# Hybrid pool / SGU / cross-attention layer on 8 cores: a new order of first loads and statistics, and four tiles of x transposed by DMA

## Chip, cores and metric

The kernel runs on the 8 cores of one Trainium2 chip. Each core computes one half (2048 rows) of one of the four sequences and no core waits for another. The metric is the device time in microseconds of the slowest core. All figures of the profile are of core 4, the slowest in the profiled execution.

## What is computed

```python
h    = rmsnorm(x, norm_pre)                       # (B, S, 2048)
proj = h @ w_in                                   # columns: xa | ga | u | v | gb | q | gc, 1024 each
ya = pool_mixer(xa) * silu(ga)
yb = u * (tril(W_s) @ layernorm(v) + b_s) * silu(gb)      # in chunks of 128 positions, 8 heads
yc = softmax(q k^T / 16) v_mem * silu(gc)                 # 4 heads, 256 memory tokens
y  = concat(rmsnorm(ya), rmsnorm(yb), rmsnorm(yc))
out = x + rmsnorm(y @ w_out, norm_post)
```

The change touches the first stage only: h, its transpose hT (kept on chip for all later projections), v = h @ w_in[:, v] and layernorm(v).

## The kernel before

A core's 2048 rows are 16 tiles of 128. On chip, memory is cut into 25 pages of 8 KB per partition. Instructions are written in program order into one list per engine; each waits for the semaphore counts of what it reads and overwrites. So a step's place in the code decides its place in its engine's queue, and a DMA starts when its queue (SP for x and all DMA transposes, POOL for weights, which are converted from f32 to bf16 under way) has come to it and its waits are met. An engine that waits holds up all that stands behind it in its own queue.

The first stage does for each tile:

- `x_load` (through `nt_load`, L292): DMA of 1 MB of x into one of four slots (tile modulo 4), from SP's queue. It waits until the tile four before has been read by `x_a`.
- `x_a` (`nt_a`): ACT squares the tile and sums it (L392), ACT takes the root (L257), DVE the reciprocal (L259), and DVE scales x by it and by the gain into a bf16 tile `xs` (L396). There are two `xs` slots, even and odd tiles.
- `x_pe` (`nt_pe`): TensorE transposes `xs` in two halves of 8 blocks (L283) into a PSUM bank; ACT copies half 0 (L410) and DVE half 1 (L413) to hT.
- `v_mm`: 32 matmuls of 512 columns (L280), as hf (column half of v, one PSUM bank each) by kh (row half of the weights) by part. The weights of v are four pages (`("v", hf, kh)`), each loaded in two halves.
- `v_ln` (L509 to L518): the statistics of v by two passes on ACT, and the normalised tile by DVE (L518). For tiles 0 to 3 this is done by halves: `v_ln_half` (ACT, L529 and L531), then `v_ln_end` (DVE L539 to L546).

Tiles 0 to 3 are interleaved by hand so that matmuls can begin on the part of the weights that has arrived. Tiles 4 to 15 are a loop: 16 matmuls of the tile, `x_pe` of the next, `x_a` of the one after, 16 matmuls, `v_ln`, and `x_load` of the tile four ahead. `x_dma` (`nt_dma`, L419) transposes by DMA from `xs` straight into hT; in this stage it is used for the 16 halo rows alone ("tile" 16); the memory tokens are transposed that way later, and blocks of softmax weights too (L1045).

`pump` loads the next weight pages of a fixed list (v, v, v, v, gb0, u0, gb1, u1, ...) while pages are free and fewer than `cap` weight pages are held. A page that was used before carries the semaphore counts of its last readers, and its load waits for those, not for the place in the code. `sgu_load` fetches 1.1 MB of small operands, `sgu_mask` (DVE L619) reads them and gives their page back, and `sgu_bias` is four small matmuls, twice.

Behind this stage (from some 154 us) come the projections of the branches, on the same hT, and the output product.

Of the kernel before, what the change touches and what calls it, by code (L numbers as in the profile page):

```python
# [153 lines left out]
def build_program():  # L154
# [142 lines left out]
    def page_bf(p):  # L297
        return vb(p * PG_B, 4096)
# [29 lines left out]
    def load_w(key, waits=()):  # L328
        p = dyn()
        if key[0] == "v":  # L330
            bs = [nbuf("w%s%d" % (key, i), p) for i in range(2)]
            for i in range(2):
                c = slice(i * 2048, (i + 1) * 2048)
                dma_pool(page_bf(p)[:, c], wp_d[W_INDEX[key]][:, c], writes=[bs[i]],
                         sem=("d_pg%d", "d_ph%d")[i] % p, waits=waits)
            wpage[key] = (p, bs)
            return
        b = nbuf("w" + str(key), p)
        dma_pool(page_bf(p), wp_d[W_INDEX[key]], writes=[b], sem="d_pg%d" % p)
        wpage[key] = (p, b)  # L340
# [13 lines left out]
    def wbuf(key):  # L354
        return wpage[key][1]
# [93 lines left out]
    for i in range(1, 4):  # L449
        nt_load(i, xrows(i))  # L450
    pump(4, waits=[xt_b[1].wtok])
    dma_sp(small[:], small_d, writes=[small_b], sem="d_c0")
# [96 lines left out]

    W1, W3, W4 = wbuf(("v", 0, 0)), wbuf(("v", 1, 0)), wbuf(("v", 1, 1))  # L550
    x_a(0)
    x_a(1)
    x_a(2)
    x_pe(0, halves=(0,))
    x_pe(1, halves=(0,))
    x_a(3)
    x_pe(2, halves=(0,))
    x_load(4, [W1[0].wtok])
    x_load(5, [W3[1].wtok])
    x_load(6, [W4[1].wtok])  # L560
    x_load(7)
    x_pe(0, halves=(1,))
    v_mm(0, 0, 0, 0)
    v_mm(1, 0, 0, 0)
    x_pe(3, halves=(0,))
    v_mm(2, 0, 0, 0)
    x_pe(1, halves=(1,))
    v_mm(3, 0, 0, 0)
    x_pe(2, halves=(1,))
    v_mm(0, 0, 0, 1)  # L570
    v_mm(1, 0, 0, 1)
    x_pe(3, halves=(1,))
    v_mm(2, 0, 0, 1)
    v_mm(3, 0, 0, 1)
    for part in range(2):
        for tt in range(4):
            v_mm(tt, 0, 1, part)
    x_a(4)
    for tt in range(2):
        v_ln_half(tt, 0)  # L580
    drop(*VN, dyn=False)
# [5 lines left out]
    x_pe(4, (7, 7), (0,))  # L587
    for tt in range(2, 4):
        v_ln_half(tt, 0)
    v_mm(0, 1, 1, 0)  # L590
    v_mm(1, 1, 1, 0)
    x_pe(4, (7, 7), (1,))
    v_mm(2, 1, 1, 0)
    for tt in range(3):
        v_mm(3, 1, tt // 2, tt % 2)
        v_mm(tt, 1, 1, 1)
        v_ln_half(tt, 1)
        v_ln_end(tt)
        if tt == 1:
            x_a(5)  # L600
    v_mm(3, 1, 1, 1)
    v_ln_half(3, 1)
    v_ln_end(3)

# [19 lines left out]
    def sgu_bias(half, b):  # L624
# [3 lines left out]
        for q in range(4):  # L628
# [3 lines left out]
                op0=ALU.mult, op1=ALU.add), reads=[bank[b], tsg_b, small_b], writes=[tsg_b])  # L632

    for tt in range(4, NTT):
        v_mm(tt, 0, 0)
        v_mm(tt, 0, 1)
        if tt == 4:
            v_mm(tt, 1, 0)
        if tt + 1 < NTT:
            x_pe(tt + 1)  # L640
        if tt + 2 <= NTT:
            x_a(tt + 2)
        if tt + 2 == NTT:
# [687 lines left out]
```

How the kernel before makes its waits and increments, by code:

```python
            def body(eng, lst=lst, own=own, e=e):  # L112
                seen = {}
                for fn, waits, tok in lst:
                    for s, v in waits:
                        if s == own and e == "pe":
                            continue
                        if seen.get(s, 0) >= v:
                            continue
                        eng.wait_ge(sems[s], v)
                        seen[s] = v
                    if fn is None:
                        continue
                    ins = fn(eng)
                    if tok is not None:
                        ins.then_inc(sems[tok[0]], 16 if tok[0] in self.is_dma_sem else 1)
```

## Time and profile before

| | us |
|---|---|
| median of 3 runs (1245.52 to 1246.02) | 1245.75 |
| the profiled execution | 1246.18 |
| its span, core 4 | 1244.6 |
| spans of the 8 cores | 1241.8 to 1244.6 |
| PE busy | 1210.0 (97%) |
| DVE, ACT, POOL busy | 488.6, 476.0, 216.6 |

Rows of a timeline read "start us, duration us, engine, line, operation, out<-in, count [idle time before it and what ended it]". An engine named SPq is the queue of SyncE, from which DMAs are issued: its duration is that of issuing, and "DMA to landing" is the time from issue until the data are there. In a row that merges several instructions the duration goes from the first to the last of them.

### The profile page before, as it was taken

How to read it: one execution, taken by the hardware profiler on the slowest of the kernel's cores; microseconds unless marked ns; L12 is line 12 of the kernel's file. 1: busy time of each engine (PE TensorE's matmuls, PEld its weight loads, DVE VectorE, ACT ScalarE, POOL GpSimd, SP SyncE). 2: the span in 40 equal slices, each digit the busy share in tenths (PEclk: the TensorE clock that was granted, in tenths of full speed). 3: DMA queues.
4: the chain of work that ended last, by engine and by line, in shares of the span. 5: the costliest groups of instructions: out<-in, count | busy, mean ns of one | idle time of the engine just before them, and what ended most of it. 6: DMA issues, size and time to landing. Idle time of an engine off the chain costs nothing.

```text
span 1244.6 us, 17796 instructions; the slowest of 8 cores (1241.8 to 1244.6 us)
## 1 busy us (share of the span) xinstructions
PE 1210.0 (97%) x6126; PEld 583.5 (47%) x6248; DVE 488.6 (39%) x784; ACT 476.0 (38%) x895; POOL 216.6 (17%) x206
## 2 busy tenths in 40 slices
PE   6989999999999999999999999999999999999997
PEld 3445444444444455555554444444444444444443
DVE  4367533422323333444443233333332544343434
ACT  4477633322221323222225555555632232222222
POOL 1000001121121011211121111111222222222222
PEclk9999999999999999999999999999999999999998
DMA  9965513653325462645535441452795583544342
GB/s 226 232 190 141 93 62 70 114 97 66 64 59 85 77 103 43 107 83 95 92 66 101 81 85 33 78 90 68 162 211 134 164 276 95 157 148 109 96 108 68
DMA packets 50938, 137.83 MB, mean 111 GB/s; under 512 B 22785, under 2 KB 35201, under 8 KB 37137
## 3 DMA queue, kind: packets, MB, share of 16 engines
q0 software_dynamic: 7632, 50.86, 25.8%
q1 hardware_dynamic: 43218, 85.83, 23.5%
q8 instruction: 51, 0.84, 0.3%
q14 instruction: 37, 0.30, 0.1%
HBM read 153.39 MB, written 29.36 MB: 147 GB/s over the span
## 4 chain that ended last, share of the span: by engine, by line
PE 92%; DMA 4%; issue 1%; DVE 1%; ACT 1%; POOL 0%; DVEq 0%; SPq 0%; ACTq 0%; POOLq 0%
PE ps L280 91%; DMA mem_pages<-w_pages 2%; DMA mem_pages<-x 2%; PE ps L283 1%; ACT mem_pages L1034 0%; ACT mem_pages L392 0%; DVE mem_pages L396 0%; POOL mem_pages L295 0%; ACT L1034 0%; DVE stat L1029 0%; DVE mem_pages L1039 0%; DVE mem_pages L1160 0%; DVE mem_pages L752 0%; ACT stat L257 0%; SPq L292 0%
## 5 line engine op out<-in xcount | busy, mean ns | idle before, releaser
L280 PE MATMUL ps<-mem_pages 128*128 128x512 bf16 (+1 forms) x5662 | 1184.5, 368 | 11.1 <-ACT mem_pages L410 1.9
L280 PEld LDWEIGHTS ps<-mem_pages 128*128 128x128 bf16 x5784 | 557.3, 98 | 622.5 <-issue 14.7
L717 POOL TENSOR_TENSOR mem_pages<-mem_pages 128x512 f32<-128x512 f32 x72 | 91.3, 1268 | 599.7 <-ACT mem_pages L710 597.2
L704 ACT ACTIVATE mem_pages<-mem_pages,small_c 128x512 bf16<-128x512 f32 x96 | 68.8, 716 | 275.7 <-DVE mem_pages L776 148.4
L1134 DVE SCALAR_TENSOR_TENSOR mem_pages<-ps,stat,mem_pages 128x512 f32<-128x512 f32 (+1 forms) x130 | 96.5, 742 | 160.5 <-PE ps L280 131.5
L1142 POOL TENSOR_TENSOR mem_pages<-mem_pages 128x512 f32<-128x512 f32 (+1 forms) x65 | 81.5, 1253 | 249.7 <-ACT jk L1138 249.7
L1138 ACT ACTIVATE jk<-mem_pages 128x512 bf16<-128x512 f32 (+1 forms) x65 | 40.5, 623 | 214.8 <-DVE mem_pages L1134 214.8
L907 DVE TENSOR_TENSOR mem_pages<-mem_pages 128x526 f32<-128x526 f32 (+3 forms) x80 | 56.1, 702 | 100.8 <-ACT mem_pages L901 95.8
L766 DVE TENSOR_TENSOR mem_pages<-ps,mem_pages 128x512 f32<-128x512 f32 x32 | 22.1, 691 | 141.2 <-PE ps L280 141.2
L752 DVE CAST mem_pages<-ps 128x512 bf16<-128x512 f32 (+1 forms) x24 | 14.4, 602 | 124.6 <-PE ps L280 121.4
L736 ACT ACTIVATE mem_pages<-ps 128x512 f32<-128x512 f32 x96 | 54.5, 591 | 22.5 <-PE ps L280 19.1
L901 ACT COPY mem_pages<-ps 128x512 f32<-128x512 f32 x32 | 18.8, 586 | 113.2 <-PE ps L280 72.1
L710 ACT ACTIVATE mem_pages<-mem_pages 128x512 f32<-128x512 f32 x96 | 58.9, 613 | 0.0
L295 POOL DMA_DIRECT2D mem_pages<-w_pages x52 | 28.7, 561 | 147.0 <-DVE mem_pages L619 81.4
L1131 ACT ACTIVATE mem_pages<-ps,stat 128x512 f32<-128x512 f32 (+1 forms) x65 | 43.6, 671 | 18.8 <-DVE mem_pages L1160 6.9
L396 DVE SCALAR_TENSOR_TENSOR mem_pages<-mem_pages,stat 128x2048 bf16<-128x2048 f32 (+1 forms) x19 | 44.6, 2350 | 2.4 <-DVE stat L259 0.5
L1160 DVE SCALAR_TENSOR_TENSOR mem_pages<-mem_pages,stat 128x2048 f32<-128x2048 f32 (+1 forms) x19 | 38.0, 2014 | 11.7 <-POOL mem_pages L1142 9.5
L392 ACT ACTIVATE mem_pages<-mem_pages 128x2048 bf16<-128x2048 f32 (+1 forms) x19 | 36.3, 1911 | 13.5 <-DMA mem_pages<-x 13.5
L1034 ACT ACTIVATE mem_pages<-ps,stat 128x256 f32<-128x256 f32 x64 | 30.4, 474 | 5.5
L283 PE MATMUL ps<-ident,mem_pages 128*128 128x128 bf16 x272 | 20.5, 230 | 10.2 <-DVE mem_pages L396 4.0
L1037 DVE RECIPROCAL stat<-stat 128x4 f32<-128x4 f32 x16 | 2.9, 178 | 66.3 <-ACT mem_pages L1034 66.3
L259 DVE RECIPROCAL stat<-stat 128x1 f32<-128x1 f32 (+2 forms) x55 | 9.1, 168 | 49.1 <-ACT stat L257 49.0
(66 smaller groups left out, 438.5 us busy)
## 6 DMA issues: line engine op xcount, KB each, us to landing
mem_pages<-w_pages POOLq DMA_DIRECT2D x44, 1024.0 KB, 14.0
mem_pages<-x SPq DMA_DIRECT2D x32, 1024.0 KB, 9.1
out<-mem_pages SPq DMA_DIRECT2D x15, 1024.0 KB, 6.2
y_scr<-mem_pages SPq DMA_DIRECT2D x96, 128.0 KB, 2.2
mem_pages<-y_scr SPq DMA_DIRECT2D x12, 1024.0 KB, 13.3
mem_pages<-w_pages POOLq DMA_DIRECT2D x8, 512.0 KB, 22.0
mem_pages<-mem SPq DMA_DIRECT2D x2, 1024.0 KB, 6.8
mem_pages<-mem_norm SPq DMA_DIRECT2D x1, 1024.0 KB
```

The lines of the kernel that those rows point to most:

```text
L280: return lambda e: e.matmul(out, lhsT=lhsT, rhs=rhs, start=start, stop=stop)
L396: P.op("dve", lambda e: e.scalar_tensor_tensor(out=xs, in0=xt, scalar=c, in1=gv, op0=ALU.mult, op1=ALU.mult), reads=[xb, gain["b"], stb], ...
L704: P.op("act", lambda e: e.activation(out=yv, in_=tmp, func=AF.Copy, scale=gbr[:, c:c + 1]), reads=[tmp_b[i], gbr_b], writes=[ring_b[r]])
L710: P.op("act", lambda e: e.activation(out=dst, in_=tmp, func=AF.Square), reads=[tmp_b[i]], writes=[dst_b])
L717: P.op("pool", lambda e: e.tensor_tensor(out=accl_v if last else acc, in0=acc, in1=dst, op=ALU.add), reads=[dst_b, acc_b[tb]], writes=[acc ...
L736: P.op("act", lambda e: e.activation(out=sil_v[i], in_=psb(b), func=AF.Silu), reads=[bank[b]], writes=[sil_b[i]])
L907: P.op("dve", lambda e, o=o, cur=cur, lo=lo, step=step: e.tensor_tensor(out=o[:, lo:528], in0=cur[:, lo:528], in1=cur[:, lo - step:528 - s ...
L1131: P.op("act", lambda e: e.activation(out=ov, in_=psb(bks[0], 0, n), func=AF.Identity, scale=sc(rc)), reads=[bank[bks[0]], rbr_b[tb]], writ ...
L1134: P.op("dve", lambda e, br=br: e.scalar_tensor_tensor(out=ov, in0=psb(bks[br], 0, n), scalar=sc(rc + br * 16), in1=ov, op0=ALU.mult, op1=A ...
L1138: P.op("act", lambda e: e.activation(out=jk_v[:, 0:n], in_=ov, func=AF.Square, scale=D ** -0.5, accum_out=sc(so)), reads=[ob], writes=[jk_ ...
L1142: P.op("pool", lambda e: e.tensor_tensor(out=ov, in0=ov, in1=gv, op=ALU.mult), reads=[ob, gp["b"]], writes=[ob])
L1160: P.op("dve", lambda e, o=o, xv=xv: e.scalar_tensor_tensor(out=o, in0=o, scalar=sc(ST_FR + tt), in1=xv, op0=ALU.mult, op1=ALU.add), reads= ...
```

## The change

1. `load_w` passes one wait to each half of a weight page. The first half of the first v page now waits for x tile 0, the second half for tile 1; before, all waited for tile 1.
2. The order of the first four tiles is new: tiles 0 and 1 are transposed whole before the rest, tiles 2 and 3 later, whole; x tile 4 is loaded after the third half page of weights has landed (before: after the first) and tile 5 after the eighth (before: after the sixth).
3. Tiles 0 and 1 get their statistics of v by `bn_stats` and `bn_aggr` on DVE instead of two passes on ACT, and are normalised in two halves.
4. Tiles 9, 11, 13, 15 are no longer transposed by TensorE. Their `x_a` comes after the `v_ln` of the tile three before, then the `x_load` of the tile four ahead of them, then the DMA transpose. The other loads stand right behind `x_a` too, so `sgu_load` now stands behind the load of tile 11.
5. gb0, the fifth weight page, waits for x tile 11. The next two pages (gb1, u1) are called for at the end of the loop only, in one `pump`.

```diff
-                         sem=("d_pg%d", "d_ph%d")[i] % p, waits=waits)
+                         sem=("d_pg%d", "d_ph%d")[i] % p, waits=waits[i:i + 1])
...
-        dma_pool(page_bf(p), wp_d[W_INDEX[key]], writes=[b], sem="d_pg%d" % p)
+        dma_pool(page_bf(p), wp_d[W_INDEX[key]], writes=[b], sem="d_pg%d" % p, waits=waits)
...
-    pump(4, waits=[xt_b[1].wtok])
+    pump(1, waits=[xt_b[0].wtok, xt_b[1].wtok])
+    pump(3)
...
+    def v_bn(tt, hf):
...
+        P.op("dve", lambda e: e.bn_stats(out=stat[:, c:c + 6], in_=psb(b)), reads=[bank[b]], writes=[stb])
+
+    def v_bn_end(tt):
...
+        P.op("dve", lambda e: e.bn_aggr(out=stat[:, mv:mv + 2],
+                                        in_=stat[:, c:c + 12].rearrange("p (a s) -> p a s", a=2)),
+             reads=[s0, s1], writes=[s1])
+        rstd_of(sc(mv + 1), sc(mv + 1), s1)
+        for hf in range(2):
+            P.op("dve", lambda e, hf=hf: e.tensor_scalar(out=vn_v(tt)[:, hf * 512:(hf + 1) * 512], in0=psb(b + hf),
...
-    W1, W3, W4 = wbuf(("v", 0, 0)), wbuf(("v", 1, 0)), wbuf(("v", 1, 1))
+    W2, W4 = wbuf(("v", 0, 1)), wbuf(("v", 1, 1))
     x_a(0)
     x_a(1)
+    for hf in range(2):
+        x_pe(0, halves=(hf,))
+        x_pe(1, halves=(hf,))
     x_a(2)
...
     x_a(3)
-    x_pe(2, halves=(0,))
-    x_load(4, [W1[0].wtok])
-    x_load(5, [W3[1].wtok])
-    x_load(6, [W4[1].wtok])
+    x_load(4, [W2[0].wtok])
+    x_load(5, [W4[1].wtok])
+    x_load(6)
     x_load(7)
...
     for part in range(2):
-        for tt in range(4):
-            v_mm(tt, 0, 1, part)
+        v_mm(0, 0, 0, part)
+        v_mm(1, 0, 0, part)
+    x_pe(2)
+    for part in range(2):
+        v_mm(2, 0, 0, part)
+    x_pe(3)
+    for tt in range(3):
+        v_mm(tt, 0, 1, 0)
+    for kh, part in ((0, 0), (0, 1), (1, 0)):
+        v_mm(3, 0, kh, part)
     x_a(4)
-    for tt in range(2):
-        v_ln_half(tt, 0)
+    for tt in range(4):
+        v_mm(tt, 0, 1, 1)
+        if tt < 2:
+            v_bn(tt, 0)
+        else:
+            v_ln_half(tt, 0)
...
+    DT = (9, 11, 13, 15)
+    x_load(8)
+    x_load(9)
     for tt in range(4, NTT):
...
-        if tt + 1 < NTT:
+        if tt + 1 < NTT and tt + 1 not in DT:
             x_pe(tt + 1)
-        if tt + 2 <= NTT:
+        if tt + 2 <= NTT and tt + 2 not in DT:
             x_a(tt + 2)
+            x_load(tt + 6)
...
         v_ln(tt)
-        if tt + 4 <= NTT:
-            x_load(tt + 4)
+        if tt + 3 in DT:
+            x_a(tt + 3)
+            x_load(tt + 7)
+            x_dma(tt + 3)
         if tt + 4 > NTT:
             drop(xt_p[tt % NX])
             if tt == NTT - 1:
                 drop(xt_p[0])
-            pump(1, cap=8)
+                pump(4, cap=8)
         if tt == 5:
             sgu_load()
         if tt == 7:
             sgu_mask()
-            pump(2)
+            pump(1, waits=[xt_b[3].wtok])
+            pump(1)
```

## Rows read from the trace of the kernel before

**Rows 1.** The page: busy time of the engines, and the chain that ended last

```profile
PE 1210.0 (97%) x6126; PEld 583.5 (47%) x6248; DVE 488.6 (39%) x784; ACT 476.0 (38%) x895; POOL 216.6 (17%) x206
PE 92%; DMA 4%; issue 1%; DVE 1%; ACT 1%; POOL 0%; DVEq 0%; SPq 0%; ACTq 0%; POOLq 0%
```

**Rows 2.** Windows: busy us (instructions) by engine, granted clock, DMA share, GB/s

```profile
60.00:65.00 5.00, 3.59 (x29) 1.90 (x27) 4.12 (x7) 2.40 (x9) 0.00 (x0) 1.00 0.93 287
65.00:70.00 5.00, 3.12 (x16) 1.39 (x15) 3.11 (x9) 4.14 (x6) 0.00 (x0) 1.00 1.01 290
...
180.00:1244.00 1064.00, 1047.80 (x5231) 502.42 (x5334) 393.00 (x638) 371.62 (x719) 209.80 (x190) 1.00 0.47 102
```

**Rows 3.** Timeline of PE, 22 to 90 us: first matmuls, the last gaps, the steady loop

```profile
22.63 3.62 PE L280 MATMUL ps<-mem_pages 128*128 128x512 bf16 x8
...
62.44 1.05 PE L283 MATMUL ps<-ident,mem_pages 128*128 128x128 bf16 x16 [1.36 <-DVE stat L539]
...
67.10 3.61 PE L280 MATMUL ps<-mem_pages 128*128 128x512 bf16 x16 [1.88 <-ACT mem_pages L410]
72.11 1.05 PE L283 MATMUL ps<-ident,mem_pages 128*128 128x128 bf16 x16 [1.40 <-DVE stat L513]
...
79.91 1.06 PE L283 MATMUL ps<-ident,mem_pages 128*128 128x128 bf16 x16
```

**Rows 4.** Weight pages of the start: POOL's timeline, and issues 16.0 to 17.1 to landing

```profile
12.62 4.96 POOL L295 DMA_DIRECT2D mem_pages<-w_pages  x9 [11.92 <-DMA mem_pages<-x]
...
L295 POOL DMA_DIRECT2D mem_pages<-w_pages x3: 580/587/596, 15.9 to 17.0; - x3
DMA to landing us min/median/max: 28.5/33.4/42.1
```

**Rows 5.** The chain and the timeline where x tile 5 arrives

```profile
41.75 15.35 DMA mem_pages<-x
...
57.19 1.91 ACT L392 ACTIVATE mem_pages<-mem_pages 128x2048 bf16<-128x2048 f32 x1 [0.60 <-DMA mem_pages<-x]
...
59.95 2.35 DVE L396 SCALAR_TENSOR_TENSOR mem_pages<-mem_pages,stat 128x2048 bf16<-128x2048 f32 x1
```

**Rows 6.** Timeline, one tile of the loop: x_a of tile 8, v_ln of tile 6

```profile
81.52 1.91 ACT L392 ACTIVATE mem_pages<-mem_pages 128x2048 bf16<-128x2048 f32 x1
...
84.28 2.35 DVE L396 SCALAR_TENSOR_TENSOR mem_pages<-mem_pages,stat 128x2048 bf16<-128x2048 f32 x1
84.51 1.02 ACT L509 ACTIVATE mem_pages<-ps 128x1024 bf16<-128x1024 f32 x1 [0.60 <-PE ps L280]
...
87.46 0.29 ACT L257 ACTIVATE stat<-stat 128x1 f32<-128x1 f32 x1 [0.62 <-DVE stat L515]
...
88.19 1.34 DVE L518 TENSOR_SCALAR mem_pages<-ps,stat 128x1024 bf16<-128x1024 f32 x1 [0.18 <-DVE stat L259]
```

**Rows 7.** L419: the DMA transpose of 128x2048 issued at 235.9

```profile
DMA to landing us min/median/max: 4.2/4.2/4.2
```

**Rows 8.** To landing: pages of 701.3/701.8, transpose, stores of 713.6/714.7, page of 796.9

```profile
DMA to landing us min/median/max: 18.0/20.5/23.0
...
L1045 SPq DMA_TRANSPOSE mem_pages<-mem_pages x1: 1757/1757/1757, 705.0 to 705.0; - x1
DMA to landing us min/median/max: 20.6/20.6/20.6
...
DMA to landing us min/median/max: 11.9/12.3/12.7
...
DMA to landing us min/median/max: 22.8/22.8/22.8
```

**Rows 9.** Issue to landing: x at 94.5, x at 102.3, weight page at 99.0

```profile
DMA to landing us min/median/max: 5.7/5.7/5.7
...
DMA to landing us min/median/max: 10.3/10.3/10.3
...
DMA to landing us min/median/max: 11.9/11.9/11.9
```

More of the change, by code:

```diff
@@ L249, in build_program @@
     ST_LH0, ST_LH1 = 352, 360
-    ST_SL = 368
+    ST_SL, ST_BN = 368, ST_SO
     ST_EPS = 383
@@ L548, in v_ln_end @@
              reads=[bank[b], bank[b + 1], s1], writes=[vn_b[tt]])
-    W1, W3, W4 = wbuf(("v", 0, 0)), wbuf(("v", 1, 0)), wbuf(("v", 1, 1))
+    def v_bn(tt, hf):
+        b = v_bank(tt, hf)
+        stb = Buf("st_bn")
+        ln_half_b[tt, hf] = stb
+        c = ST_BN + 12 * tt + 6 * hf
+        P.op("dve", lambda e: e.bn_stats(out=stat[:, c:c + 6], in_=psb(b)), reads=[bank[b]], writes=[stb])
+    def v_bn_end(tt):
+        b = v_bank(tt, 0)
+        s0, s1 = ln_half_b[tt, 0], ln_half_b[tt, 1]
+        c = ST_BN + 12 * tt
+        mv = ST_LH0 + 2 * tt
+        P.op("dve", lambda e: e.bn_aggr(out=stat[:, mv:mv + 2],
[4 more added lines that the diff above has]
+            P.op("dve", lambda e, hf=hf: e.tensor_scalar(out=vn_v(tt)[:, hf * 512:(hf + 1) * 512], in0=psb(b + hf),
+                                                         scalar1=sc(mv), scalar2=sc(mv + 1), op0=ALU.subtract,
+                                                         op1=ALU.mult),
+                 reads=[bank[b + hf], s1], writes=[vn_b[tt]])
@@ L551, in build_program @@
+    W2, W4 = wbuf(("v", 0, 1)), wbuf(("v", 1, 1))
     x_a(0)
     x_a(1)
+    for hf in range(2):
+        x_pe(0, halves=(hf,))
+        x_pe(1, halves=(hf,))
     x_a(2)
-    x_pe(0, halves=(0,))
-    x_pe(1, halves=(0,))
     x_a(3)
-    x_pe(2, halves=(0,))
-    x_load(4, [W1[0].wtok])
-    x_load(5, [W3[1].wtok])
-    x_load(6, [W4[1].wtok])
+    x_load(4, [W2[0].wtok])
+    x_load(5, [W4[1].wtok])
+    x_load(6)
     x_load(7)
-    x_pe(0, halves=(1,))
-    v_mm(0, 0, 0, 0)
-    v_mm(1, 0, 0, 0)
@@ L565, in build_program @@
[L565 to L574, printed above, removed]
-    for part in range(2):
-        for tt in range(4):
-            v_mm(tt, 0, 1, part)
-    x_a(4)
-    for tt in range(2):
-        v_ln_half(tt, 0)
+    for part in range(2):
+        v_mm(0, 0, 0, part)
[3 more added lines that the diff above has]
+        v_mm(2, 0, 0, part)
@@ L587, in build_program @@
     x_pe(4, (7, 7), (0,))
-    for tt in range(2, 4):
-        v_ln_half(tt, 0)
     v_mm(0, 1, 1, 0)
@@ L593, in build_program @@
     v_mm(2, 1, 1, 0)
-    for tt in range(3):
-        v_mm(3, 1, tt // 2, tt % 2)
+    for kh, part in ((0, 0), (0, 1), (1, 0)):
+        v_mm(3, 1, kh, part)
+    for tt in range(2):
+        v_mm(tt, 1, 1, 1)
+        v_bn(tt, 1)
+        v_bn_end(tt)
+    x_a(5)
+    for tt in range(2, 4):
         v_mm(tt, 1, 1, 1)
@@ L598, in build_program @@
         v_ln_end(tt)
[L599 to L603, printed above, removed]
     wt = {}
```

## The prediction

> **What bounds the kernel now.** I read the page's busy times and chain first [rows 1]: TensorE is busy 97% of the span and is 92% of the chain, so only two things move the time: work taken from TensorE, and idle time of TensorE filled or made. The windows then say where the idle time is [rows 2]: before the matmuls start at 22.63, and between 60 and 70 us (3.59 and 3.12 busy of 5.00 each), while the 1064 us from 180 on hold 16 us of idle in many small pieces, which the change doesn't touch. The DMA engines are full there (share 0.93 and 1.01). Third, the timeline of PE [rows 3]: the matmuls start at 22.63; the last gaps of the first stage are 1.36, 1.88 and 1.40 us, ahead of 62.44, 67.10 and 72.11; from 73.00 on PE runs without a gap, a tile every 7.8 us (72.11 to 79.91), of which the 16 transposes take 0.89 (72.11 to 73.00) and the 32 matmuls 6.91. Fourth, the cause of the three gaps [rows 5]: x tile 5 was issued at 41.75 and needed 15.35 us; ACT waited for it until 57.19, the scaled tile was ready at 59.95 + 2.35 = 62.30, and the gaps at 67.10 and 72.11 are the statistics and copies queued behind it on ACT and DVE. From 72 us on the loop is bound by TensorE alone: its loads, ACT and DVE run ahead.
>
> **The change part by part.**
>
> *First loads.* Nine weight DMAs are issued back to back from 12.62 [rows 4]. Eight are the halves of the v pages; the ninth, whole, is gb0: its page is free, so it is issued at 17.0 and lands at 17.0 + 42.1 = 59.1, long before it is needed, and shares the engines with x tile 5. The eighth half (issued 16.5) lands at 16.5 + 33.4 = 49.9. After the change gb0 waits for x tile 11 and x tile 5 is issued behind the eighth half instead of beside the last two. Halves issued before took some 3.5 us each in a full queue ((41.5 - 17 - 3.6 for x tile 4) / 6, where the sixth, issued 15.4 with 26.1 to landing, came at 41.5), while the last two took 8.4 together: 1.4 us of that was x tile 5. Without it, and with the early start of the first half page in engines that weren't quite full at 7 to 11 us, the eighth lands at about 48.2. A load of x alone takes 5.7 [rows 9], up to 6.4 for those issued near 79: x tile 5 lands at 48.3 + 6.1 = 54.4, 2.7 earlier than 57.1.
>
> Does TensorE reach that point in time? Tiles 0 and 1 are bound by the gain's copies on DVE as before (tile 0's scale starts at 12.50); x tiles 1 to 3, which landed at 12.0, 15.6 and 18.9, now share the engines with weights and come later, tile 3 at up to 26 by equal shares. By my count matmuls start at 21.7 instead of 22.6, lose 2 us at x_pe(2) and x_pe(3) (nothing stands between a transpose and the matmuls that need its copy), and have tiles 0 to 3 done at 55.9 instead of 55.2. Tile 4's 24 matmuls follow to 61.1. x tile 5 is scaled at 54.4 + 5.1 (from the start of L392 at 57.19 to 62.30) = 59.5, and the queue of statistics on ACT behind it (tiles 2 and 3 still go by ACT) has the same length as before: 67.10 becomes 64.4 and 72.11 becomes 69.4. Gain 2.7 us. Bounds: nothing, if tile 3 of x is so late that TensorE ends its four tiles 3 us later; 5.5, if TensorE has the three gaps filled besides.
>
> *bn_stats.* No trace shows one. It reads 128x512 of PSUM, between nothing and twice a DVE copy of that form (0.69 us each for the gain): four of them 2.8 us on a DVE that is idle for 8.7 us before 48.17. ACT loses four pairs of passes of 1.6 us. Both lie beside matmuls and ahead of x tile 5, on which ACT waits anyway: 0, from -0.5 to +1.
>
> *Transposes off TensorE.* Four times 0.89: -3.6 us, if nothing takes their place.
>
> *The DMA transposes.* A transpose of this size took 4.2 us from issue to landing on quiet engines [rows 7]. When is it issued and due? Take tile 9. The v_ln of tile 6 starts at 84.51 - 2.7 = 81.8; its root is at 87.46 - 2.7 = 84.8, done 85.1 [rows 6]. Then x_a(9): 5.1 us from L392 to the end of L396 (81.52 to 86.63), so 90.2. SP then issues the load of x tile 13 first and the transpose at 90.6. Due: tile 6's matmuls end at 81.6, tile 7 takes 7.8 with x_pe(8), tile 8 takes 6.9, the bias matmuls 0.4: 96.7. That leaves 6.1 us, enough for 4.2 alone.
>
> But it isn't alone. (a) One queue is worked in order: the two stores issued at 713.6 and 714.7 behind a transpose took 11.9 to 12.7 instead of the 2.2 of their kind, landing just behind it [rows 8]. The transpose of tile 9 stands behind 1 MB of x, which takes 5.7 alone and took 10.3 beside a weight page [rows 9]. gb0 is such a page: it waits for x tile 11, issued 78.9 - 2.7 and landed 6.4 later = 82.6, and is under way to about 95. So x tile 13 lands at 90.2 + 10.3 = 100.5. (b) A transpose beside weight pages waits for their end: that of 705.0 took 20.6 instead of 3.1 (10 of its 14 kind) and landed at 725.6, when the last of three pages issued from 700.75 on had landed at 701.8 + 23.0 = 724.8; the one of 800.2 likewise took 20.6 and landed 1.1 behind a page issued at 796.9 with 22.8 to landing. u0 needs the page that sgu_mask gives back: v_ln of tile 7 ends at 88.19 + 1.34 + 7.8 - 2.7 = 94.6, the mask takes 1.2, issue at 96.2, landing 11.9 later at 108.1 [rows 9]. Tile 9's transpose can start at 100.5, in the middle of that. It lands about 1.0 behind the page: 109.1. TensorE stands still from 96.7 to 109.1: +12.4. Bounds: 2.2, if x tile 13 lands in 5.7 and the transpose 3 us behind; 13.5.
>
> In the DMA view such a transpose is some 2100 packets and a weight page 216 (1728 for eight). The Trainium skill, DMA: Bandwidth & Descriptors, "Queues, rings and completion order", says that each DMA engine turns between its queues a packet at a time; by this rule the transpose would get little before the page is through, and the trace agrees with its 20.6 us.
>
> After so long a pause TensorE begins again at the lower clock. The first 8 matmuls of the run took 3.62 us, 0.43 apart, against 0.22 in the loop [rows 3], which is 512 columns at 1.2 and at 2.4 GHz, though the granted clock reads 1.00 there. Eight of them: +1.7, from 0 to 1.7; the gaps of 1.9 cost no such thing.
>
> Tile 11 uses the same xs slot, so its L392 on ACT waits for tile 9's transpose, and x_pe(10)'s copy stands behind it on ACT. It is scaled at 109.1 + 5.1 = 114.2, x tile 15 lands 5.7 later, the transpose at 123; due 109.1 + 7.8 + 6.9 + 0.4 = 124.2. No stall, with 1 us in hand. Tile 13 has no load ahead of it: scaled 8.4 behind the end of tile 10, due 14.7 behind it, 6.3 in hand for 4.2. But gb1 isn't held to the stage's end: its pump stands later in the code, while it takes the page of x tile 13 as before and waits only for that tile's last reader, which is L396(13) itself. Page and transpose are issued within 0.5 us of each other. The page's data start 1.6 us after its issue (at 126.6 before), the transpose's after 1.2, so it has 1 of its 2.9 us done and the rest falls behind the page: 0.5 to its issue, 1.6 to its data, 7.0 for two halves of 3.5, 1.5 for what is left of the transpose, less the 6.3 in hand: +4.3, bounds 0 and 6.1 (0.5 + 11.9 - 6.3, [rows 9]). Tile 15 then finds u1 nearly through: 0, at most 2.
>
> Sum: -2.7 + 0 - 3.6 + 12.4 + 1.7 + 4.3 = +12.1. Against the profiled execution's 1246.2: 1258.3. That execution lay 0.4 over the median, so 1258. Later stages run on TensorE at 97% and shift as a whole; gb0 to u1 have landed well before they use them.
>
> **Rivals.** *The transposes are hidden.* If pages and transposes run beside each other without loss, all four land within their 6 us. It would need x tile 13 and the transpose to pass ahead of the page. For it: in 10 of 14 cases of L1045 nothing disturbed. Against it: the two of 20.6, and the fact that the load ahead alone takes 5.7 of the 6.1. Time 1246.2 - 6.3 = 1239.9: this is the case on the other side, and it decides when the transpose lands before 96.7. The Trainium skill, Advanced Engine Details and Errata, "X-Bar Transpose (TRN2)", speaks for it: transposing DMAs are as fast as regular ones, 350 GB/s and more, an estimate of 1.5 us for these 0.5 MB; the trace's 4.2 us on quiet engines disagrees already. *Order without starvation.* The transpose only waits for the x load ahead and shares fairly: tile 9 lands between 98.9 and 103.4, stall 2.2 to 6.7, tile 13 none: 1242 to 1249, middle 1244.8. The weight streams in rows 8 were three deep, here one, which speaks for it; work that must pass the engines between 82 and the landing (sgu 3.5, gb0 at least 6.7, two x tiles 7.2, the transpose 2.9) speaks against less than 4. *The start gets worse as well.* x tiles 2 and 3 come later than 26 us, in-order TensorE stands before x_pe(3), the weights gain nothing by it, and the first term is +1 to +4 instead of -2.7: 1262 to 1265.
>
> **How the numbers follow.** Forecast with its bounds, 1250 to 1263: 57%. Hidden: 14%. Order without starvation: 19%. A worse start on top: 10%. About 0.2% (2.5 us) is what a measurement of this kernel tells from no change. Faster by more: 14 + 3 = 17%. Within: 13% of the second rival. Slower: 57 + 10 + 3 = 70%. The range leaves out most of the hidden case and the end of the last: 1243 to 1264.
>
> **What would show it.** Right: the gaps on PE ahead of 67 and 72 us come 2 to 3 us earlier; PE has one gap of some 12 us before tile 9's matmuls near 96, ended by a DMA; the transpose of tile 9 shows 15 us or more to landing, and that of tile 13 some 10; 12 instead of 16 groups of transposes in the stage. Wrong: landings of 4 to 6 us for all four; a first matmul later than 24; x tile 5 landing after 57.

## The result, and the profile after

The changed kernel took 1310.15 us (median of 5 runs; before 1245.75, of 5 as well): 1.0498 of before, 95% interval 1.0475 to 1.0521. The forecast was 1258, range 1243 to 1264. The sign was right, the size was missed by 52 us. In some executions, whatever the kernel, the cores of a die run at a lower granted clock (0.81 in the one of 1511.79 us here), and all ratios are without these.

The spans of the eight cores lie between 1278.2 and 1304.3 us (before 1241.8 to 1244.6). The page of the slowest, core 1: its busy times and its chain that ended last:

```profile
PE 1217.7 (93%) x6184; PEld 580.5 (45%) x6184; DVE 489.1 (37%) x782; ACT 467.9 (36%) x875; POOL 216.2 (17%) x206
PE 88%; DMA 7%; ACT 2%; DVE 2%; issue 1%; DVEq 0%; SPq 0%; ACTq 0%; POOLq 0%
```

Against [rows 1], TensorE went from 97 to 93% busy and DMA from 4 to 7% of the chain. The list of waits of PE, with total, times and longest, says why:

```profile
PE ps L280 <- DMA mem_pages<-mem_pages: 59.0, 2, 38.2
```

These are two waits of together 59.0 us for a DMA from SBUF to SBUF, which is the DMA transpose. The timeline of PE, core 1, shows where:

```profile
20.94 3.57 PE L280 MATMUL ps<-mem_pages 128*128 128x512 bf16 x8 [0.70 <-DMA mem_pages<-w_pages]
...
63.09 1.05 PE L283 MATMUL ps<-ident,mem_pages 128*128 128x128 bf16 x16 [1.89 <-DVE stat L540]
...
67.75 3.61 PE L280 MATMUL ps<-mem_pages 128*128 128x512 bf16 x16 [1.88 <-ACT mem_pages L410]
72.76 1.05 PE L283 MATMUL ps<-ident,mem_pages 128*128 128x128 bf16 x16 [1.40 <-DVE stat L514]
...
99.61 0.39 PE L280 MATMUL ps<-mem_pages,ones_bf 128*128 128x128 bf16 x4
138.23 5.71 PE L280 MATMUL ps<-mem_pages 128*128 128x512 bf16 x16 [38.24 <-DMA mem_pages<-mem_pages]
...
190.84 5.01 PE L280 MATMUL ps<-mem_pages 128*128 128x512 bf16 x16 [20.72 <-DMA mem_pages<-mem_pages]
```

The gap of 38.24 stands ahead of tile 9, that of 20.72 ahead of tile 13; tiles 11 and 15 wait for nothing. What was under way on the DMA side, from the timelines of SP's queue and of POOL:

```profile
93.87 22.96 SPq L419 DMA_TRANSPOSE mem_pages<-mem_pages  x1
...
143.81 5.31 SPq L419 DMA_TRANSPOSE mem_pages<-mem_pages  x1
...
164.08 2.11 SPq L419 DMA_TRANSPOSE mem_pages<-mem_pages  x1
...
87.25 0.53 POOL L295 DMA_DIRECT2D mem_pages<-w_pages  x1 [71.67 <-DMA mem_pages<-x]
99.67 0.53 POOL L295 DMA_DIRECT2D mem_pages<-w_pages  x1 [11.88 <-DVE stat L259]
164.53 0.53 POOL L295 DMA_DIRECT2D mem_pages<-w_pages  x1 [64.34 <-ACT mem_pages L510]
```

The POOL rows are gb0, u0 and gb1. From issue to landing, tile 9's transpose (issued 93.87) and u0 (issued 99.67) took:

```profile
DMA to landing us min/median/max: 44.2/44.2/44.2
...
DMA to landing us min/median/max: 38.1/38.1/38.1
```

They land together, at 138.1 and 137.8, and both are stretched: a transpose on quiet engines takes 4.2 [rows 7], a page with one load of x beside it 11.9 [rows 9]. They weren't alone. gb0 (issued 87.25) took 15.1 and landed at 102.4, and the load of x tile 13, issued at 93.49 ahead of the transpose in its queue, took 16.4 and landed at 109.9. Issuing the transpose kept SP busy for 22.96 us, so the next load of x was issued at 117.05 only. Tile 13's transpose and gb1 took 26.6 and 26.3, and u1 was issued beside them, in 23.6:

```profile
117.05 26.71 SPq L292 DMA_DIRECT2D mem_pages<-x  x2
...
172.09 0.53 POOL L295 DMA_DIRECT2D mem_pages<-w_pages  x1 [7.04 <-DVE mem_pages L396]
```

Tile 11's transpose, at 143.81 with no page beside it, landed in 7.4. The windows of the first gap (span, busy us by engine, granted clock, DMA share, GB/s) show the collapse:

```profile
110.00:120.00 10.00, 0.00 (x0) 0.00 (x0) 0.00 (x0) 0.00 (x0) 0.00 (x0) 0.50 1.29 56
120.00:130.00 10.00, 0.00 (x0) 0.00 (x0) 0.00 (x0) 0.00 (x0) 0.00 (x0) 0.50 1.80 73
130.00:140.00 10.00, 1.77 (x5) 0.68 (x6) 0.00 (x0) 1.77 (x1) 0.00 (x0) 0.50 0.33 103
```

Packets are under way all the time (the share adds up the times of all packets, so it can pass 1: 1.29 and 1.80 from 110 to 130), yet only 56 and 73 GB/s are moved, where the kernel before moves 287 at a share of 0.93 [rows 2]. No engine computes from 110 to 130. The granted clock reads 0.50, which is 1.2 GHz, and the first matmuls after the gap go at the lower level: tile 9's sixteen take 5.71 instead of the 3.61 of the same form [rows 3], tile 13's 5.01.

The account of the two profiled executions closes. The spans differ by 1304.3 - 1244.6 = 59.7. The gaps are 38.2 + 20.7 = 58.9; the slow matmuls 2.1 + 1.4 = 3.5; the start is 0.65 late (72.76 against 72.11 [rows 3]); four transposes off TensorE give back 3.6. Sum 59.5. The other cores show the same in other sizes: the two gaps together are 33 to 59 us.

### The profile page after: what moved, and what is told of

Same layout as the page of the kernel before. It is cut to its first block, busy times and chain, and to the rows that moved or that the text cites. A ratio compares the mean times of both kernels' runs of the same rounds, so it can differ in the third digit from the quotient of the medians.

```text
span 1304.3 us, 17755 instructions; the slowest of 8 cores (1278.2 to 1304.3 us)
## 1 busy us (share of the span) xinstructions
PE 1217.7 (93%) x6184; PEld 580.5 (45%) x6184; DVE 489.1 (37%) x782; ACT 467.9 (36%) x875; POOL 216.2 (17%) x206
## 4 chain that ended last, share of the span: by engine, by line
PE 88%; DMA 7%; ACT 2%; DVE 2%; issue 1%; DVEq 0%; SPq 0%; ACTq 0%; POOLq 0%
PE ps L280 87%; DMA mem_pages<-mem_pages 5%; DMA mem_pages<-w_pages 1%; DMA mem_pages<-x 1%; ACT mem_pages L392 1%; DVE mem_pages L396 1%; PE ps L283 1%; ACT mem_pages L1062 0%; ACT L1062 0%; ACT stat L257 0%; DVE stat L1057 0%; ACT mem_pages L510 0%; ACT mem_pages L512 0%; DVE mem_pages L1067 0%; ACT mem_pages L410 0%
## 5 line engine op out<-in xcount | busy, mean ns | idle before, releaser
L280 PE MATMUL ps<-mem_pages 128*128 128x512 bf16 (+2 forms) x5784 | 1195.9, 369 | 65.5 <-DMA mem_pages<-mem_pages 59.0
L764 ACT ACTIVATE mem_pages<-ps 128x512 f32<-128x512 f32 x96 | 54.5, 591 | 21.9 <-PE ps L280 18.4
L392 ACT ACTIVATE mem_pages<-mem_pages 128x2048 bf16<-128x2048 f32 (+1 forms) x19 | 36.2, 1905 | 64.3 <-DMA mem_pages<-mem_pages 52.1
L903 DVE SCALAR_TENSOR_TENSOR mem_pages<-ps,small_c,mem_pages 128x512 f32<-128x512 f32 x32 | 22.5, 745 | 8.0 <-PE ps L280 8.0
```

The costliest lines, as they stand in the source:

```text
L280: return lambda e: e.matmul(out, lhsT=lhsT, rhs=rhs, start=start, stop=stop)
L392: P.op("act", lambda e: e.activation(out=sqo, in_=xt, func=AF.Square, scale=D ** -0.5, accum_out=c), reads=[xb], writes=[sqb, stb])
L764: P.op("act", lambda e: e.activation(out=sil_v[i], in_=psb(b), func=AF.Silu), reads=[bank[b]], writes=[sil_b[i]])
```

## The experiments

**Which part of the change.** First the changed kernel with no tile transposed by DMA, then the kernel before with nothing but the four DMA transposes.

```
-    DT = (9, 11, 13, 15)
+    DT = ()
```

> The changed kernel with all 16 tiles transposed by TensorE; the new first part and the waits of the weight pages stay. Theory 'the early part is worth nothing, its new wait takes the place of the old' (the last gap of the changed kernel's first part ends at 72.76 instead of 72.11, because ACT's root for tile 1's statistics stands ahead of x tile 5): +0.6 us, 1246.4. The forecast's theory 'x tile 5 lands earlier and all shifts': 1243.1. If the early part were itself to blame for the 64 us: above 1290.

Measured: 1249.82, ratio 1.0024 (1.0014 to 1.0034). By the ratios the whole change costs 62 us (0.0498 x 1247). 3 of them are there without any DMA transpose; the other 59 appear only with the transposes.

> The kernel before with the four DMA transposes alone (its first part, statistics and weight pages unchanged: gb0 is through at 59, u0 is issued near 99). Theory 'a weight page and a DMA transpose in flight together stretch each other' : tile 9's transpose, issued near 93 behind x tile 13, meets u0 and again takes 25 us or more, u0 25 or more instead of 11.9; 1270 to 1310. Theory 'the transpose only waits for the page, which keeps its 11.9' (the forecast's): 1256 to 1260. Theory 'it takes gb0 and u0 both, back to back': 1240 to 1250 here.

Measured: 1282.15, ratio 1.0278 (1.026 to 1.0296): this part alone makes the larger half of the loss, 35 us. The remaining 24 need transposes and the rest of the change together. Where they lie can be seen: the gap ahead of tile 9 is 1.2 to 8.8 us here and was 24.1 to 38.2 in the changed kernel, whose gb0 had been held back until it was still under way when the transpose was issued (here it landed at the start). No run changes that alone. In the profiled execution the even cores have spans of 1251.5 to 1257.6, the odd ones of 1277.6 to 1279.9. Core 1, PE's timeline:

```profile
108.46 5.43 PE L280 MATMUL ps<-mem_pages 128*128 128x512 bf16 x16 [8.45 <-DMA mem_pages<-mem_pages]
...
165.35 5.99 PE L280 MATMUL ps<-mem_pages 128*128 128x512 bf16 x16 [25.28 <-DMA mem_pages<-mem_pages]
```

And from issue to landing, the pair issued at 133.80 (transpose of tile 13) and 134.25 (gb1):

```profile
DMA to landing us min/median/max: 31.4/31.4/31.4
...
DMA to landing us min/median/max: 31.5/31.5/31.5
```

No load of x is anywhere near that pair. The next page, u1, is issued at 142.05, in the middle of it, so the 31 us aren't the price of one page and one transpose. But the collapse is there before u1. Windows of core 1, with nothing but the pair under way:

```profile
138.00:140.00 2.00, 2.00 (x10) 0.74 (x8) 1.29 (x3) 0.69 (x3) 0.00 (x0) 1.00 3.67 92
140.00:142.00 2.00, 0.07 (x1) 0.00 (x0) 1.51 (x1) 1.74 (x3) 0.00 (x0) 1.00 0.78 26
```

26 GB/s are moved from 140 to 142 (22 and 32 on cores 3 and 7), and the transpose, 8.2 us under way at 142, would have landed at 138.0 with its 4.2 us. A page and a transpose are enough to start it; how long the pair would have taken without u1, this run doesn't say.

**Is it the page?** The changed kernel with the pages kept away: gb0 at the start again, and u0, gb1 and u1 not before tile 15's transpose has landed.

```
-                pump(4, cap=8)
+                pump(4, cap=8, waits=[hT_b[15][0].wtok])
...
         if tt == 7:
             sgu_mask()
-            pump(1, waits=[xt_b[3].wtok])
             pump(1)
```

> The changed kernel with gb0 loaded at the start as before, and u0, gb1, u1 really held until the transpose of tile 15 has landed. Theory 'weight pages beside transposes': all four land in 4 to 12 us, TensorE has no gap before tiles 9 and 13, and only u0 comes late (transpose 15 lands near 147, the page 11.9 later, needed near 154: a stall of about 4): 1244 to 1250. Theory 'the load of x ahead in the same queue and the width of the transpose' : tile 9's transpose takes 20 us and more again; 1280 to 1310.

Measured: 1252.94, ratio 1.0042 (1.0025 to 1.006). The transposes land in 4.2 to 8.9 us, and the gap ahead of tile 9 is 1.2 to 2.8. Some 57 of the 62 us are gone with the pages. The interval is not below that of the kernel without DMA transposes, so with the new start the transposes off TensorE (3.6 us) didn't show as a gain. On core 4, the slowest, the gap of 2.80 and its slow matmuls (5.13 for sixteen instead of 3.61) cost more than that; on six cores the gap is 1.2 to 1.9 with 3.61 behind it.

**Does the transpose's size, or its place in its queue, matter?** Each transpose as two of 1024 columns; and the transpose issued ahead of the load of x instead of behind it.

```
+        for hf in range(2):
+            P.op("sp", lambda e, hf=hf: e.dma_start_transpose(
+                out=hTv[i // 4][hf][:, :, (i % 4) * 128:(i % 4 + 1) * 128], in_=xs[:, hf * 1024:(hf + 1) * 1024]),
+                reads=[xsb], writes=[hT_b[i][hf]], dma_sem=("d_tr%d", "d_tu%d")[hf] % (i % 2))
```

> The changed kernel with each DMA transpose as two of 1024 columns, the form of L1045 that landed 0.8 and 1.1 us behind the last weight page in the kernel before, without stretching the page. Theory 'the 2048-column form makes the trouble': u0 keeps 12 to 15 us, tile 9's transpose lands near 112, 1255 to 1265. Theory 'any transpose that shares the engines with a page for long does': as the changed kernel, 1290 to 1315, u0 over 25 us to landing.

Measured: 1292.84, ratio 1.035 (1.0281 to 1.0418), gaps ahead of tile 9 of 21.2 to 31.3 us. Halves don't slip through. They cost less than the whole ones, though (1.035 against 1.0498, the intervals are apart), and why is open.

```
             x_a(tt + 3)
-            x_load(tt + 7)
             x_dma(tt + 3)
+            x_load(tt + 7)
```

> The changed kernel with one swap: the transpose of tiles 9, 11 and 13 is handed to its queue ahead of the x load four tiles on instead of behind it. Theory (pages and transpose drag each other out, whatever stands in the transpose's own queue): gaps ahead of tile 9 of 25 to 40 us remain and the time is 1290 to 1315. Rival (the forecast's own step: the transpose is late because it stands behind 1 MB of x, and starts in the middle of u0): the transpose starts at 94, before u0's page is handed back, lands at 98 to 104, the gap is under 8 us and the time is 1250 to 1262.

Measured: 1299.16, ratio 1.0428 (1.039 to 1.0465). The time is the theory's, the cores are split: ahead of tile 9, cores 1, 2, 4 and 7 have 6.6 to 7.3 us, which is what the rival gave, core 5 has 18.0 and cores 0, 3 and 6 have 25.7 to 31.6. All of them lose 8.3 to 27.0 more at tile 13, where nothing was swapped. So the load ahead in the queue was part of it on half of the cores; on core 3 the transpose issued at 95.27 took 38.0, beside gb0 (issued 90.9, 13.8 to landing) and u0 of 101.44 with 34.5.

**One page and one transpose.** As c_held, but the transposes stand ahead of the loads of x, gb0 is issued when tile 9 is scaled, with its transpose, and no other page is near (the lines are against the changed kernel):

```
+            t9 = xs_slot(tt + 3)[1].wtok
+            x_dma(tt + 3)
             x_load(tt + 7)
-            x_dma(tt + 3)
+            if tt == 6:
+                pump(1, waits=[t9])
```

> The disputed cost by itself: the changed kernel with exactly one weight page (gb0) issued in the moment of tile 9's transpose, which stands ahead of the load of x; all other pages held until the transpose of tile 15 has landed. Theory 'starvation alone' (the forecast's): page 11 to 12 us, transpose 12 to 13 us to landing, gap before tile 9 some 6 us. Theory 'they stretch each other': both 18 us or more, gap 12 or more, TensorE back at the lower clock.

Core 0's timelines of SP's queue, POOL and PE:

```profile
94.62 2.07 SPq L419 DMA_TRANSPOSE mem_pages<-mem_pages  x1
...
95.08 0.53 POOL L295 DMA_DIRECT2D mem_pages<-w_pages  x1 [78.37 <-DVE mem_pages L396]
...
123.92 6.01 PE L280 MATMUL ps<-mem_pages 128*128 128x512 bf16 x15 [22.78 <-DMA mem_pages<-mem_pages]
```

From issue to landing, the transpose and the page:

```profile
DMA to landing us min/median/max: 29.2/29.2/29.2
...
DMA to landing us min/median/max: 28.2/28.2/28.2
```

The profiled execution took 1270.4. One after the other the two would be 4.2 + 11.9 = 16 us; side by side the transpose takes 23.2 to 29.2 and the page 22.0 to 28.2 over the eight cores, with gaps of 16.8 to 22.8. The loss is a joint one, not a matter of who goes first. The next transpose, without a page, landed in 4.3.

The pair isn't quite alone here either: two loads of x stand behind the transpose in SP's queue, issued at 96.86 and 102.9. They aren't the cause by themselves. In best7_again below, loads of x stand behind the transposes in the same way with no page near, and the transposes land in 4.2 to 9.2; and a page with a load of x but no transpose takes 11.9, the load 10.3 [rows 9]. It takes a transpose and a page; how much the loads of x add to the 28 us isn't measured.

The next kernel is g_one_page with a plain copy of 1 MB of x, issued from POOL, in the page's place (a spare transfer that nobody reads):

```
-                pump(1, waits=[t9])
+                jp = dyn()
+                dma_pool(page_f(jp), x_d[0:128, :], writes=[nbuf("jp", jp)], sem="d_jk", waits=[t9])
+                drop(jp)
```

> As g_one_page, with the page's place taken by a copy of 1 MB of x without conversion, from the same queue (POOL); all four pages come after the transpose of tile 15, so the next stage waits for gb0 some 8 us. Theory 'any other queue beside the transpose': both as long as in g_one_page. Theory 'it is the conversion from f32 to bf16, 2 MB read for 1 MB written in 216 packets': the copy under 10 us, the transpose under 10.

Measured: 1286.25 in the profiled execution, whose pages come late for the next stage, so that the total says nothing here. Core 0: transpose 18.3 us, copy 17.6, gap 11.94; over the eight cores 16.3 to 19.5, 15.4 to 19.3 and 7.5 to 13.1, all below those of g_one_page. The weight page isn't special, then, and its conversion isn't needed; a plain copy from POOL's queue does it too, less strongly. Both are 144 packets in the DMA view (the 216 of the forecast, from the eight halves of the start, were too many); the page reads 2 MB of float32 and writes 1 MB, the copy reads and writes 1 MB. What makes it 28.2 us for a page and 17.6 for a copy is thus not the number of packets.

**Does it happen anywhere?** Three versions of the kernel before with four spare pairs each beside the second stage: a weight page and a DMA transpose from hT, into two pages that nobody reads. The first has transposes of 128x1024, half the size, the second of 128x2048, the third both. Each ran once; what counts is the landings, not the time.

> The kernel before, with four spare pairs of transfers added in the second stage (their results are not used; weight pages there are loaded at most four ahead): a weight page into a spare page, and a DMA transpose of 128x1024 from hT. Pair 1: both at once, the transpose written in steps of 1 KB (the form of the changed kernel's halves). Pair 2: both at once, written without gaps (the form of L1045). Pair 3: the page some 4 us ahead, without gaps. Pair 4: the page some 4 us ahead, in steps. Theory 'the destination's steps make the trouble': pairs 1 and 4 take 20 us and more, pairs 2 and 3 leave the page its 11 to 12 us and land 1 behind it. Theory 'who comes first': pairs 1 and 2 over 20, pairs 3 and 4 11 to 13. Theory 'any overlap': all four over 20.

Measured: 1247.02 beside 1247.07. The pairs overlapped less than meant. Page 1.4 us behind the transpose: 3.1 to 6.1 and 10 to 12 us. Page 5.7 ahead: 4.4 to 7.0 and 8.7 to 11.2.

> Again spare transfers beside the second stage, into two pages that nobody reads, but each transpose is now 128x2048, as large as one of the change's. Pairs 1 and 2 (heads 3 and 4) have the transpose issued some 1.4 us ahead of the weight page, pair 1 into blocks 256 columns apart as the kernel's, pair 2 into contiguous blocks; pairs 3 and 4 (heads 5 and 6) have the page ahead, by under 1 us and by 1 to 4 us. Theory (a page that arrives while a transpose of this size is under way collapses with it, whatever the place in the kernel): pairs 1 and 2 show both landings at 17 to 30 us, pair 3 perhaps as well, pair 4 a transpose that lands just behind its page (9 to 12 us) and a page of 10 to 12. Rival (the collapse needs the first stage's surroundings, such as the x loads in transposing form or the slow engines there): all pages 10 to 12 and no transpose over 12. If it hangs on the target's step between blocks, pair 1 is stretched and pair 2 is not. Time within 0.5% of before in each case, since nothing waits for the spare transfers.

Measured: 1247.36. No transpose over 11.5, no page over 13.3: the theory missed by a factor of two. The text on record says there that blocks 256 columns apart are as the kernel's; the kernel's are 512 apart, which is one more reason for the next kernel.

> Spare pairs beside the second stage once more. t_micro2's pairs differed from the kernel's in two ways: the page was issued 1.4 us behind the transpose instead of 0.45, so that the transpose was more than half through, and its target's blocks lay 256 columns or none apart, where the kernel's lie 512 apart. Pair 1: two transposes of 128x1024 into blocks 512 columns apart, page 0.5 us behind. Pair 2: one of 128x2048 into contiguous blocks, page 0.5 behind. Pair 3: as pair 1, page 1.4 behind. Pair 4: 128x2048 into blocks 256 apart, page 0.5 behind. If the overlap in time is what makes a page and a transpose stretch each other: pairs 1, 2 and 4 land at 17 to 30 us both, pair 3 at 8 to 9 and 12 to 13. If it is the step of 512 columns: pairs 1 and 3 at 17 to 30, pairs 2 and 4 under 10 and 14. If it is something of the first stage's surroundings: none above 14. Time within 0.5% of before.

Measured: 1248.01. The pair nearest to the kernel's, a 128x2048 with a page issued 0.9 us behind it (core 0, transpose and page):

```profile
DMA to landing us min/median/max: 12.0/12.0/12.0
...
DMA to landing us min/median/max: 13.0/13.0/13.0
```

Over the eight cores no transpose of 128x2048 took over 12.4, and the pages of the four pairs took 10.1 to 13.6. The pair is through in no more than the time of one after the other (16 us); there is waiting, but no collapse. The halves of this kernel are written in the form of e_tr_halves, 512 columns apart, and none took over 10.9, so the step of the target is not what makes 28 us of it. The distance in time came down to 0.9 us only, where the kernel's is 0.45. Something of the first stage's surroundings does it, and which it is stays open: these pairs have no load of x and no second page near, another source page, and engines that do other work at the time. The windows of b_dma_tr_only show that the first two aren't needed to start it. Whether the transfers of the other cores, which are at the same place of the same stage at nearly the same time, have a part in it was not tested.

**The start.** Two kernels on the forecast's first term. The kernel before with gb0 held back until x tile 11:

```
-        dma_pool(page_bf(p), wp_d[W_INDEX[key]], writes=[b], sem="d_pg%d" % p)
+        dma_pool(page_bf(p), wp_d[W_INDEX[key]], writes=[b], sem="d_pg%d" % p, waits=waits)
...
-            pump(2)
+            pump(1, waits=[xt_b[3].wtok])
+            pump(1)
```

> The kernel before with one edit, gb0 waits for x tile 11. Theory of the forecast 'x tile 5 lands earlier and all behind it shifts by as much': x tile 5 near 51, 2 us or more faster. Theory 'ACT had only 0.60 us of idle time there, as its row says; the roots and passes of tiles 0 and 1 stand ahead of x tile 5': L392 for it starts 0.6 earlier, 0 to 0.6 us faster, that is the same.

Measured: 1246.73, ratio 0.9995 (0.9986 to 1.0005). x tile 5, issued at 42.4, landed 8.8 later = 51.2 instead of 57.1. ACT's timeline, core 4:

```profile
56.68 0.29 ACT L257 ACTIVATE stat<-stat 128x1 f32<-128x1 f32 x1 [1.12 <-DVE stat L543]
56.88 1.89 ACT L392 ACTIVATE mem_pages<-mem_pages 128x2048 bf16<-128x2048 f32 x1
```

5.9 us earlier on the chip, 0.31 earlier at L392 (57.19 [rows 5]): ACT had its root of tile 1 to do first. The tail "[0.60 <-DMA mem_pages<-x]" in [rows 5] said so: ACT had stood idle for 0.60 us, not for 2.7. What had run until then, the root of tile 1, stands in the timeline of ACT in the kernel before:

```profile
56.29 0.29 ACT L257 ACTIVATE stat<-stat 128x1 f32<-128x1 f32 x1 [1.12 <-DVE stat L543]
```

The second asks whether the order or bn_stats costs the 3 us: a_no_dma_tr with ACT's statistics for tiles 0 and 1.

```
-        if tt < 2:
-            v_bn(tt, 0)
-        else:
-            v_ln_half(tt, 0)
+        v_ln_half(tt, 0)
...
-        v_bn(tt, 1)
-        v_bn_end(tt)
+        v_ln_half(tt, 1)
+        v_ln_end(tt)
```

> The changed kernel without DMA transposes (as a_no_dma_tr, which gave 1.0024 of before and gaps of 1.88, 1.87 and 1.40 us ahead of 65.1, 69.8 and 74.8) and with the statistics of tiles 0 and 1 on ACT again instead of bn_stats. If the order of the first loads alone is what costs the 3 us, the ratio is 1.002 to 1.0035 again and the gap ahead of x_pe(6) is at 74 to 76 us. If bn_stats on DVE is what holds tile 5 (the root of tile 1 waits 3 us for DVE there), this is faster than a_no_dma_tr by 1 to 3 us: 1.000 to 1.0015, with the gap ahead of x_pe(6) at 72 to 73. If ACT becomes the queue that is late, it is slower by 1 to 3 us: 1.004 to 1.005.

Measured: 1252.14, ratio 1.004 (1.0026 to 1.0053), x_pe(6) at 76.23 on core 4. Without bn_stats it is later by 1.4 us in that row than a_no_dma_tr (74.80), and by 2.2 in the mean of the eight cores (76.4 and 74.3; 71.5 in the kernel before). The intervals of the two ratios overlap, so it is these rows that say it: bn_stats gains some 2 us in this order. k_gb0_held shows that holding gb0 back costs nothing, so what costs is the new order of loads, transposes and matmuls. In a_no_dma_tr, core 4, one sees with what:

```profile
25.62 3.57 PE L280 MATMUL ps<-mem_pages 128*128 128x512 bf16 x8 [1.10 <-DMA mem_pages<-w_pages]
...
33.91 13.98 PE L280 MATMUL ps<-mem_pages 128*128 128x512 bf16 x64
...
65.13 1.05 PE L283 MATMUL ps<-ident,mem_pages 128*128 128x128 bf16 x16 [1.88 <-DVE stat L540]
...
69.78 3.61 PE L280 MATMUL ps<-mem_pages 128*128 128x512 bf16 x16 [1.87 <-ACT mem_pages L410]
74.80 1.05 PE L283 MATMUL ps<-ident,mem_pages 128*128 128x128 bf16 x16 [1.40 <-DVE stat L514]
```

The matmuls start earlier (20.95 against 22.63) but wait 1.10 us for the next half page, and the eight behind that wait go at 0.43 us each again. With 24 matmuls done the long stretch of 64 begins at 33.91, in the kernel before at 31.47: 2.4 of the 2.7 us are lost by then. All three gaps of [rows 3] are there, the first even longer, and 72.11 has become 74.80.

**A version that beats both.** The kernel before, with its own start; the DMA transposes ahead of the x loads; sgu_load ahead of x tile 9 and the mask after tile 4, so that u0's page is through by then; gb1 and u1 held until transpose 15 has landed. First with tiles 9, 11, 13 and 15:

> The kernel before, its first part and statistics unchanged, with tiles 9, 11, 13, 15 transposed by DMA, and no weight page in flight beside them: the small operands are fetched ahead of x tile 9 and their page is given back after tile 4, so u0 is issued near 76 and through by 90; gb1 and u1 wait for the transpose of tile 15; each transpose stands ahead of the load of x. Theory 'only weight pages beside transposes cost': each lands in 4 to 8 us, no gap on TensorE, 4 x 0.89 = 3.6 us faster than before, ratio 0.997. Theory 'a transpose costs TensorE its time even alone, by loads of x or ports': 1247 or more.

Measured in one execution: 1246.11, beside 1246.42 and 1247.48 of the kernel before; there is no interval, and the 3.6 us that were expected are neither shown nor refuted. Then with all of tiles 9 to 15:

```
+    DT = (9, 10, 11, 12, 13, 14, 15)
...
+        if tt + 3 in DT:
+            x_a(tt + 3)
+            x_dma(tt + 3)
+            x_load(tt + 7)
...
+                pump(4, cap=8, waits=[hT_b[15][0].wtok])
```

> The same with the seven tiles 9 to 15 transposed by DMA. Theory 'only weight pages beside transposes cost': 7 x 0.89 = 6.2 us faster than before, ratio 0.995. Against it, theory 'the queue fills': a load of x (3.6 us of the engines) and a transpose (2.9) come every 6.9 us up to x tile 15, so each lands later than the last and TensorE waits 1 to 3 us at tiles 10 to 12: ratio 0.997 to 1.001.

> The kernel of best7 once more, since most runs of its call were disturbed and gave no interval. 6.2 us faster than before: ratio 0.995.

Measured: the first time 1240.66 in one execution; the second time ratio 0.9948 (0.993 to 0.9967), lowest 1240.17, spans of 1236.3 to 1239.8. The longest gap left behind 80 us in the stage, on any core, is on core 1:

```profile
108.56 151.76 PE L280 MATMUL ps<-mem_pages 128*128 128x512 bf16 x746 [1.05 <-DMA mem_pages<-mem_pages]
```

Seven times 0.89 = 6.2 us were to be had, 6.5 were measured (0.0052 x 1247; 4.1 to 8.7 by the interval). The transposes land in 4.2 to 9.2 us. Then gb0 held as well, and tile 5 scaled one tile earlier on ACT:

> As best7, and gb0 waits for x tile 7, and x_a(5) stands one tile earlier, ahead of tile 1's statistics. Theory 'the queues of ACT and DVE set the last gaps': the gap before x_pe(5) goes (1.4 us), those behind it stay in part; 1 to 1.5 us faster than best7, 7 to 8 faster than before, ratio 0.994.

Measured: 0.995 (0.9932 to 0.9969), no better. The gap ahead of x_pe(5) went from 1.86 to 0.65 on the cores read, the two of 1.87 and 1.40 behind it stayed.

## Why the forecast was wrong

*The place of the stalls and who meets whom: right.* The forecast put one stall ahead of tile 9, by its transpose beside u0 and behind x tile 13, and one ahead of tile 13, by gb1 issued within 0.5 us of the transpose (0.45 measured); tiles 11 and 15 free. All that is in the rows above, and c_held shows that without the pages the stalls are gone.

*The size of the stalls: the step that failed.* "It lands about 1.0 behind the page: 109.1" took the page's 11.9 us as given and let the transpose pay alone: "(b) A transpose beside weight pages waits for their end". The page itself took 38.1. With that measured value the forecast's own rule gives 99.67 + 38.1 + 1.0 = 138.8, against 138.1. So the end of the transpose at the end of the page was right here (in the pair of b_dma_tr_only it landed 0.6 ahead of the page); what was wrong was that the page keeps its time. The terms 12.4, 1.7 and 4.3, together 18.4, measured 38.2, 3.5 (for both gaps) and 20.7 on core 1, together 62.4. The load of x tile 13 was priced too low as well: 16.4 us beside gb0 instead of 10.3. In [rows 8] there was already a page with 22.8 to landing beside a transpose; I read it as a page among others, which it was, the last of three, and priced the page by its quiet neighbour of [rows 9]. The bound of 13.5 was built with the same 11.9, and so was no bound.

The Trainium skill, DMA: Bandwidth & Descriptors, "Rules for kernel authors", says that a transpose next to ordinary DMAs needs nothing done. That row is about correct results and names no time; the time is another matter here: g_one_page measures 29.2 and 28.2 us for a transpose and a page that take 4.2 and 11.9.

*First loads, -2.7: wrong in sign.* The landings came even better than forecast: the eighth half at 15.0 + 31.2 = 46.2 (forecast 48.2), x tile 5 at 46.4 + 4.9 = 51.3 (54.4). But L392 of tile 5 ran at 57.84, right behind tile 1's root, which had waited 3.12 us for DVE. The step that failed is "ACT waited for it until 57.19", taken as if all of the 2.7 us were waiting for the DMA; k_gb0_held shows 0.31 of it. What the new order costs was a rival of the forecast with 10%, "the start gets worse as well" (+1 to +4): a_no_dma_tr measured +3.0 (0.0024 x 1247), though by waits for half pages rather than for x tiles 2 and 3.

*bn_stats, 0, from -0.5 to +1: outside its range, on the good side.* Four took 0.69 us each, within what was assumed; in this order they save ACT the passes on which tile 5 waits, some 2 us by the rows of the two kernels without DMA transposes.

*Transposes off TensorE, -3.6: right*, and in best7_again it is seen as a time: 6.5 us for seven.

*The lower clock, +1.7: nearly right for one gap.* The sixteen matmuls behind the two long gaps took 5.71 and 5.01 instead of 3.61, which is 2.1 and 1.4 more: by 0.21 us each that makes an estimated ten and seven slow ones. There were two such gaps, and the forecast counted one.

*The rivals.* "The transposes are hidden" is what c_held and best7_again make true by other means: no page near. "Order without starvation" would have the transposes share fairly; it fell with g_one_page, where the transpose stood ahead in its queue and the gap was 16.8 to 22.8 us.

## What to carry to other kernels

Two transfers that share the DMA engines have a joint price, and it can be above the sum of the two: where a row shows one of them long beside the other (22.8 for 11.9), the quiet row is no bound for either, and here even the long one was too small (28.2, up to 38.1). Before a wait is given a value, read the idle time in the row of the waiting instruction: what its engine did until then doesn't come any earlier. In this kernel DMA transposes that replaced work on the bottleneck paid (6.5 us for seven) once the large transfers of the other queue were kept away until they had landed.

## What was not expected of the hardware

- A DMA transpose of 0.5 MB and a weight page of 1 MB side by side, from two queues, in the first stage: 29.2 and 28.2 us (4.2 and 11.9 apart), with gb0 and a load of x besides up to 44.2 and 38.1. A like pair beside the second stage: 12.0 and 13.0. What tells the two places apart is not known.
- A plain 1 MB copy from POOL's queue does it too: 18.3 and 17.6 us.
- It can split the cores of one execution: with the four transposes alone, the odd cores' spans are 24 us longer in the mean than the even ones', and in d_tr_first the gap ahead of tile 9 is either about 7 us or 18 to 32.
- While both are under way the DMA engines show a share of 1.29 to 1.80 and move 56 to 73 GB/s (core 1, 110 to 130 us).
